# First output product started inside the last attention items; shift, gate and final rows loaded by SP before the experts

## The chip, the cores and the metric

The kernel runs on one core of one Trainium2 chip. The metric is the device time of one execution in microseconds (us). Engines: PE is TensorE (matmuls and transposes), DVE VectorE, ACT ScalarE, POOL GpSimd, SP SyncE. SP computes nothing; it issues DMAs.

## What is computed

Two decoder layers over 640 tokens: 512 latent tokens of a sample and 128 prompt tokens, width 1024. Cut to what matters here (one layer, from the reference):

```
h = _rmsnorm(x, P['norm_mix_g'][l]) * (1 + scm) + sm
a, own = _mixer(h, l, P, pos, ctx)          # differential attention, 4 heads, and latent attention, 4 heads
x = x + gm * a                              # a = mixed @ P['w_o'][l], the output projection
h = _rmsnorm(x, P['norm_ffn_g'][l]) * (1 + scf) + sf
f = _swiglu(h, ...) if l % 2 == 0 else _moe(h, ...)   # layer 1: 8 experts, top 2
x = x + gf * f
```

At the end `y = _rmsnorm(x, final_norm_g)`. The six rows sm, scm, gm, sf, scf, gf (shift, scale and gate) come out of the condition vector, one set for the latent tokens and one for the prompt. All matmul operands are float32, split into a high and a low part, so that each product is three matmuls.

## The kernel before

The program is written out by hand: one block per engine, each a fixed list of instructions with waits on semaphores. The activations of the trunk are kept transposed (features on partitions, tokens along the row). Matmul results go to PSUM, of which three regions of 1024 columns ("main", at 0, 1024 and 2048) are handed out in turn by the table that `plan()` (L212) writes, and a fourth (3072) serves the rest. `claim_main` makes PE wait until the result three places earlier in the table has been read.

**Attention.** Each layer runs two attentions, f = 0 (differential) and f = 1 (latent), of 17 items each (`N_ITEMS`): an item is one head of one tile of 128 queries, and one item takes all four heads of the prompt tile. For an item PE computes scores (L2414), DVE their maximum, ACT the exponentials (L1151, `exp_done`), PE transposes them (L2435, `tr_done`), ACT copies them out (L1197, `pt_ready`), PE multiplies them by the values (L2449, `pv_done`), and ACT copies the result out with its scale (L1173, `pv_evac`). The loop in PE's `attention` (L2459) keeps two items ahead with the scores and issues for item i the values of item i-1 and then the transposes of item i. Of f = 1 all items put the transposes into columns 2048 to 2815 and the values behind them (`turned_at`, `values_at`), so that each waits for the one before to be copied out.

When the items of a query tile are done, `turn_out` (L2553) turns its heads, ACT and DVE split them into `h_hi` and `h_lo` (L1225, L1770, `o_split`). Ten such turns fill the eight k chunks of h: chunks 0 to 3 are the differential heads, which are ready after the first five turns, early in f = 1; chunks 4 to 7 are the latent heads, complete after the last turn (L2583), which follows item 16.

**Output projection.** Then come eight products ("o", l, d), one for each 128 output features (L2601 to L2603). `split_both` (L2284) runs over the 8 chunks of k, three operand pairs and two halves of 320 tokens: 48 matmuls. Before them PE waits for the last turn to be split, and fills that wait: in layer 0 with two throw-away matmuls (`keep_busy`, L2178), in layer 1 with 32 small matmuls that spread the FFN's shift rows over all partitions (L2597); ACT copies these to SBUF (L1245, `shift_row`). After each product DVE adds the gated result to x (L1606), ACT takes squares and scales, and both split the weight of the product after next (L1005, L1456).

**Router and experts.** After the last product of layer 1 come the router, the transposed tokens, to which DVE adds the shift rows (L1959), and the tables of slots. The experts run as 17 slots of 128 tokens; each slot streams 18 pieces of up to 1 MB of weights through nine buffers (SP, L801), which ACT and DVE split (L1334, L2013) for PE (L2708 to L2710). SP issues piece n + 9 when piece n has been split. In the last slot POOL loads `fin_row` (the final norm's weight, L965) and the first gate row (L966), gathers ten blocks of slot results (L971), and loads the second gate row (L975). DVE's `update` (L2113) and `last_norm` (L2122) end the program, one token tile after the other.

## Time and profile before

| | us |
|---|---|
| median of 3 runs | 2054.04 (2053.56 to 2054.39) |
| the profiled execution's own time | 2051.91 |
| its span in the trace | 2050.3 |
| first attention item of layer 0 to the end of the output products of layer 1 | 161 to 1168 |
| router and tables | 1168 to 1200 |
| 17 expert slots | 1200 to 2022 |
| final updates and output | 2022 to 2050 |

PE is busy 97% of the span, DVE 75%, ACT 56%, POOL 12%. The table of the page that divides the span into 40 slices shows PE at nine tenths or more in nearly all of them, and DMA at nine tenths or more in all slices of the experts. A stage is therefore read from its own stretch: in which few places PE stands still, and what it runs there that is not part of the result.

### The profile page before, as it was taken

The page shows a single profiled execution, that of the slowest core. Times are in us where ns is not written, and L with a number is a line of the kernel's source. Part 1 is how long each engine was busy: PE and PEld are TensorE (multiplying, and loading weights), DVE is VectorE, ACT ScalarE, POOL GpSimd, SP SyncE. Part 2 cuts the span into 40 slices and gives each one's busy share as a digit, 9 for nine tenths or more (in the row PEclk, how much of TensorE's full clock was granted, in tenths as well). Part 3 has the DMA queues.
Part 4 walks back from the last instruction along what each step waited for, and adds up shares of the span by engine and source line. Part 5 has one row for each costly group of instructions (what it writes and reads, how often), then busy time and mean ns, then how long its engine had stood idle before and what let it go on. Part 6 is the DMA issues. An engine that isn't in the chain of part 4 may idle for free. (4 is left out here: it accounts for less than half of the span.)

```text
span 2050.3 us, 31301 instructions
## 1 busy us (share of the span) xinstructions
PE 1996.1 (97%) x11814; PEld 1775.3 (87%) x11814; DVE 1528.1 (75%) x1709; ACT 1140.7 (56%) x1389; POOL 239.2 (12%) x258
## 2 busy tenths in 40 slices
PE   8999999999999999999999989999999999999997
PEld 4898679999999999989878978888888888888884
DVE  5547676877767775755852479988899988989997
ACT  5217663322212223623864368777778878788774
POOL 1130100000000000121100037000000000100012
PEclk9999999999999999999999999999999999999999
DMA  9220432344453443321000089999999999999995
GB/s 340 77 90 6 146 113 93 114 164 149 134 169 134 155 132 96 125 69 67 1 1 22 7 325 385 386 386 386 386 386 386 386 386 387 386 387 386 386 387 203
DMA packets 267136, 447.17 MB, mean 218 GB/s; under 512 B 12993, under 2 KB 159393, under 8 KB 266881
## 3 DMA queue, kind: packets, MB, share of 16 engines
q1 hardware_dynamic: 246048, 375.74, 51.7%
q0 software_dynamic: 19120, 67.84, 9.1%
q10 hardware_dynamic: 1872, 2.26, 0.3%
q8 instruction: 67, 1.10, 0.2%
q14 instruction: 29, 0.23, 0.0%
HBM read 430.29 MB, written 16.63 MB: 218 GB/s over the span
## 5 line engine op out<-in xcount | busy, mean ns | idle before, releaser
L2013 DVE TENSOR_TENSOR w_lo<-mraw,w_hi 128x1792 fp32r<-128x1792 f32 (+2 forms) x306 | 643.3, 2113 | 89.0 <-ACT w_hi L1334 86.4
L1334 ACT ACTIVATE w_hi<-mraw 128x1792 fp32r<-128x1792 f32 (+2 forms) x306 | 541.6, 1775 | 174.0 <-PE ps L2710 156.7
L2708 PE MATMUL ps<-w_hi,xs_lo 128*128 128x448 f32 (+1 forms) x816 | 310.0, 380 | 4.8 <-DVE w_lo L2013 3.6
L2710 PE MATMUL ps<-w_hi,xs_hi 128*128 128x448 f32 (+1 forms) x816 | 305.0, 374 | 0.0
L2709 PE MATMUL ps<-w_lo,xs_hi 128*128 128x448 f32 (+1 forms) x816 | 304.7, 373 | 0.0
L1456 DVE TENSOR_TENSOR sub_lo<-zone,sub_hi 128x1024 fp32r<-128x1024 f32 (+2 forms) x112 | 128.3, 1147 | 152.0 <-ACT sub_hi L1005 151.8
L2708 PEld LDWEIGHTS ps<-w_hi,xs_lo 128*128 128x128 f32 x816 | 153.3, 188 | 30.2 <-DVE w_lo L2013 11.2
L2710 PEld LDWEIGHTS ps<-w_hi,xs_hi 128*128 128x128 f32 x816 | 153.2, 188 | 19.2
L2709 PEld LDWEIGHTS ps<-w_lo,xs_hi 128*128 128x128 f32 x816 | 153.4, 188 | 17.8
L2284 PE MATMUL ps<-f_hi,sub_lo 128*128 128x320 f32 x704 | 162.2, 312 | 0.7 <-DVE sub_lo L1456 0.7
L2284 PE MATMUL ps<-f_hi,sub_hi 128*128 128x320 f32 x704 | 161.5, 310 | 0.0
L1005 ACT ACTIVATE sub_hi<-zone 128x1024 fp32r<-128x1024 f32 (+2 forms) x112 | 108.9, 974 | 94.2 <-PE ps L2299 93.7
L2284 PE MATMUL ps<-f_lo,sub_hi 128*128 128x320 f32 x704 | 160.8, 309 | 0.0
L2708 PE MATMUL ps<-w_hi,ea_lo 128*128 128x512 f32 x374 | 151.1, 404 | 2.5 <-DVE w_lo L2013 2.5
L2710 PE MATMUL ps<-w_hi,ea_hi 128*128 128x512 f32 x374 | 146.8, 392 | 0.0
L2709 PE MATMUL ps<-w_lo,ea_hi 128*128 128x512 f32 x374 | 146.3, 391 | 0.0
L1703 DVE TENSOR_REDUCE stat<-ps 128x2 f32<-128x1536 f32 (+2 forms) x68 | 90.5, 1334 | 59.9 <-PE ps L2414 57.3
L2284 PE MATMUL ps<-h_hi,sub_lo 128*128 128x320 f32 x528 | 121.9, 312 | 4.7 <-DVE sub_lo L1456 4.1
L2284 PE MATMUL ps<-h_hi,sub_hi 128*128 128x320 f32 x528 | 121.7, 311 | 0.0
L2284 PE MATMUL ps<-h_lo,sub_hi 128*128 128x320 f32 x528 | 121.6, 311 | 0.0
L2284 PEld LDWEIGHTS ps<-f_hi,sub_lo 128*128 128x128 f32 x704 | 119.3, 189 | 0.9 <-issue 0.9
L2284 PEld LDWEIGHTS ps<-f_lo,sub_hi 128*128 128x128 f32 x704 | 119.7, 189 | 0.0
(368 smaller groups left out, 3667.8 us busy)
## 6 DMA issues: line engine op xcount, KB each, us to landing
mraw<-in_moe_w_down SPq DMA_DIRECT2D x68, 1024.0 KB, 14.5
mraw<-in_moe_w_gate SPq DMA_DIRECT2D x68, 896.0 KB, 13.0
mraw<-in_moe_w_up SPq DMA_DIRECT2D x68, 896.0 KB, 13.1
in_cos<-in_w_mods POOLq DMA_DIRECT2D x72, 512.0 KB, 3.7
mraw<-in_moe_w_gate SPq DMA_DIRECT2D x34, 1024.0 KB
mraw<-in_moe_w_up SPq DMA_DIRECT2D x34, 1024.0 KB
mraw<-in_moe_w_down SPq DMA_DIRECT2D x34, 768.0 KB, 14.7
zone<-in_w_in SPq DMA_DIRECT2D x13, 1024.0 KB, 5.2
```

The source lines that it names most:

```text
L1005: nc.scalar.activation(sub_of(HI, q), raw_w, ACT.Copy).then_inc(t_hi, 1)
L1334: nc.scalar.activation(w_hi[:, n % SPLITS, a], mraw[:, n % MRING, a], ACT.Copy).then_inc(w_hi_ready, 1)
L1456: nc.vector.tensor_tensor(sub_of(LO, q), raw_w, sub_of(HI, q).bitcast(f32), ALU.subtract).then_inc(t_split, 1)
L1703: nc.vector.tensor_reduce(to, sc[..., 0:nk], AXX, ALU.min).then_inc(max_ready, 1)
L2013: nc.vector.tensor_tensor(w_lo[:, n % SPLITS, a], mraw[:, n % MRING, a], w_hi[:, n % SPLITS, a].bitcast(f32), ALU.subtract).then_inc(w_spl ...
L2284: ins = nc.tensor.matmul(ps[:, o + 512 * half:o + 512 * half + wide], a[:, k - k0, :], b[:, k, TH * half:TH * half + wide], start=k == 0 a ...
L2708: nc.tensor.matmul(out, a_lo, b_hi, start=start, stop=False)
L2709: nc.tensor.matmul(out, a_hi, b_lo, start=False, stop=False)
L2710: return nc.tensor.matmul(out, a_hi, b_hi, start=False, stop=stop)
```

## The change

- The first output product ("o", l, 0) no longer runs in one piece. `first_out(k0, k1)` issues the chunks k0 to k1 of it: chunk 0 beside item 14, chunk 1 after the last item, chunks 2 and 3 after the last turn, chunks 4 to 7 when the last turn is split. It owns the main region at 1024 in both layers (`left_out` entries in the table).
- The transposes of item 16 are issued one step earlier, beside item 15, and into columns 0 to 767, its values behind them. They no longer wait for the copies of items 14 and 15. ACT copies them out right after those of item 15 (`turned`).
- The filler of layer 0 and the 32 shift matmuls of layer 1 with ACT's two copies are gone. SP stores the two shift rows to DRAM as four-byte elements, waits for them, and loads each spread over 128 partitions.
- SP loads both gate rows into `in_cos` (free once layer 1's rotary embedding is done) and `fin_row` after the last output product. POOL's three loads and its wait are gone; DVE waits for all of them once, at the first update.

```diff
-        if l:
-            for c in range(2):
-                m(("shift_row", c), "shift_row_ready", c + 1)
+        while len(main_freed) % 3 != 1:
+            left_out()
...
+    shift_rows = nc.dram_tensor("shift_rows", (2, D_MODEL), f32).ap()
...
-        gate_row = [xs, zone[:, xs_at:xs_at + D_MODEL]]
+        gate_row = [in_cos[:, c * D_MODEL:(c + 1) * D_MODEL] for c in range(2)]
...
-        def turned_at(f):
-            return 3072 if f == 0 else 2048
-
-        def values_at(f, lat):
-            return turned_at(f) + 768 if lat else ADA_AT
+        def turned_at(f, i=0):
+            return 3072 if f == 0 else 0 if i == N_ITEMS - 1 else 2048
+
+        def values_at(f, lat, i=0):
+            return turned_at(f, i) + 768 if lat else ADA_AT
...
+            for c in range(2):
+                sp.dma_start(shift_rows[c].rearrange("(k p) -> p k", p=P), mod[:, 1, 24:32, c], allow_slow_non_contiguous=True).then_inc(shift_rows_moved, 16)
+            sp.wait_ge(shift_rows_moved, 32)
+            sp.wait_ge(pv_evac, items_before(DEPTH, 0))
+            for c in range(2):
+                sp.dma_start(shift_row[c], shift_rows[c].partition_broadcast(P)).then_inc(shift_rows_moved, 16)
+            sp.wait_ge(rope_done, 9 * DEPTH)
+            sp.wait_ge(cond_gates, 48)
+            for c in range(2):
+                sp.dma_start(gate_row[c], gate_rows[c].partition_broadcast(P)).then_inc(rows_in, 16)
+            sp.wait_ge(main_done, MAIN[("o", 1, KC - 1)] + 1)
+            sp.dma_start(fin_row, d["fin"]).then_inc(rows_in, 16)
             sp.wait_ge(slots_ready, 1)
-            sp.wait_ge(main_done, MAIN[("o", 1, KC - 1)] + 1)
             e0 = expert(0)
...
             pool.dma_start(yslots[s * P:(s + 1) * P, :], ybuf).then_inc(y_stored, 16)
             pool.wait_ge(y_stored, 16 * (s + 1))
             pool.sem_inc(y_left, 1)
-            pool.wait_ge(cond_gates, 48)
-            pool.wait_ge(etr_done, 2 + G_ETR + 5 * s + TR_OF["xb"] + 1)
             pool.wait_ge(xs_in, 16 * (SLOTS - 1))
-            pool.dma_start(fin_row, d["fin"]).then_inc(rows_in, 16)
-            pool.dma_start(gate_row[0], gate_rows[0].partition_broadcast(P)).then_inc(rows_in, 16)
             pool.wait_ge(row_at_ready, 1)
...
-            pool.wait_ge(pc_done, pieces_done(SLOTS - 1, EPIECE_AT["up", 2, 4]))
-            pool.dma_start(gate_row[1], gate_rows[1].partition_broadcast(P)).then_inc(prompt_gate_in, 16)
-            pool.wait_ge(prompt_gate_in, 16)
...
+                    def turned(i):
+
+                        nt, o = 6 if item(f, i)[2] else len(item(f, i)[1]), turned_at(f, i)
+                        nc.scalar.activation(pt_buf[:, i % 2, 0:nt, :], ps[:, o:o + nt * P].rearrange("p (k n) -> p k n", k=nt),
+                                             ACT.Copy).then_inc(pt_ready, 1)
...
-                        nt = 6 if item(f, i)[2] else len(item(f, i)[1])
+                        if f and i == N_ITEMS - 1:
+                            values_out(i - 1)
+                            continue
                         act.wait_ge(tr_done, it + 1)
                         if i:
                             values_out(i - 1)
-                        o = turned_at(f)
-                        nc.scalar.activation(pt_buf[:, i % 2, 0:nt, :], ps[:, o:o + nt * P].rearrange("p (k n) -> p k n", k=nt),
-                                             ACT.Copy).then_inc(pt_ready, 1)
+                        turned(i)
+                        if f and i == N_ITEMS - 2:
+                            act.wait_ge(tr_done, it + 2)
+                            turned(i + 1)
...
                 q = SUB_AT[("o", l, 0)]
                 turned_hi(1, M_TILES[-1], N_TURN - 1)
-                if l:
-                    for c in range(2):
-                        act.wait_ge(main_done, MAIN[("shift_row", c)] + 1)
...
             def add_shift(t):
                 dve.wait_ge(htok_scaled, t + 1)
-                dve.wait_ge(shift_row_ready, 2)
-                nc.vector.tensor_tensor(htok[:, t, :], htok[:, t, :], shift_rows[t], ALU.add).then_inc(htok_ready, 1)
+                dve.wait_ge(shift_rows_moved, 64)
...
                             pe.wait_ge(exp_done, it + 1)
-                        if i:
+                        last = f and i == N_ITEMS - 1
+                        if i and not last:
                             pe.wait_ge(pt_ready, it)
-                        if i > 1:
...
                         if f and i == 0:
                             pe.wait_ge(vm_ready, 2 * l + 1)
...
                         qt, heads, lat = item(f, i)
                         pe.wait_ge(pt_ready, it + 1)
-                        if i:
+                        if i and not (f and i == N_ITEMS - 1):
                             pe.wait_ge(pv_evac, it)
...
                             if f == 0 and i == D_LAT:
                                 latent_keys(1)
-                        transposes(i)
+                        if not f or i < N_ITEMS - 1:
+                            transposes(i)
                         if i == 0 and f:
                             values_ready()
                         beside(i)
+                        if f and i == N_ITEMS - 2:
...
+                    if i == N_ITEMS - 3:
+                        pe.wait_ge(exp_done, items_before(l, 1) + N_ITEMS - 1)
+                        claim_main(("o", l, 0))
+                        pe.wait_ge(o_split, N_TURN * l + TT)
+                        first_out(0, 1)
+
+                def first_out(k0, k1):
+                    return split_both(("o", l, 0), [p[:, k0:k1, :] for p in split_sub(("o", l, 0))], h_hi, h_lo, k0, k1, KC)
 
                 attention(1, last_value_rows, lambda: pe.wait_ge(vm_early, 2 * l + 2), beside, first)
+                first_out(1, 2)
                 turn_out(1, M_TILES[-1], N_TURN - 1)
-
-
-                pe.wait_ge(exp_done, items_before(l + 1, 0))
-                pe.wait_ge(pv_evac, items_before(l + 1, 0))
-                if l == 0:
-                    keep_busy(("o", l, 0), 2, x_t[:, 0, :])
-                else:
-
-                    pe.wait_ge(mod_rows, 2 * len(MODS))
-                    for c in range(2):
-                        claim_main(("shift_row", c))
-                        o = 1024 * (MAIN[("shift_row", c)] % 3)
-                        for k in range(KC):
-                            ins = nc.tensor.matmul(ps[:, o + k * P:o + (k + 1) * P], mod[:, 1, 24 + k, c:c + 1].to_broadcast([P, P]), ident[:],
-                                                   start=True, stop=True)
-                        ins.then_inc(main_done, 1)
+                first_out(2, 4)
                 pe.wait_ge(o_split, N_TURN * (l + 1))
-                for d_ in range(KC):
+                first_out(4, KC).then_inc(main_done, products(("o", l, 0)))
+                for d_ in range(1, KC):
                     claim_main(("o", l, d_))
                     split_both(("o", l, d_), split_sub(("o", l, d_)), h_hi, h_lo, 0, KC, KC).then_inc(main_done, 1)
```

How it moves the instructions, at the places that matter. PE at the end of layer 1's second attention (L2449 values, L2435 transposes, L2553 the turn, L2597 the shift rows, L2284 the product), from the values of item 14 on:

```order
L2449 MATMUL ps<-zone 128x128 [waits pv_evac,pt_ready]
L2449 MATMUL ps<-zone 128x128 x5
L2435 MATMUL ps<-ident,zone 128x128 [waits pv_evac,pt_ready,exp_done]
L2435 MATMUL ps<-ident,zone 128x128 x5
L2553 MATMUL ps<-ident,zone 128x128 [waits pv_evac,o_split]
L2553 MATMUL ps<-ident,zone 128x128 x3
L2449 MATMUL ps<-zone 128x128 [waits pv_evac,pt_ready]
L2449 MATMUL ps<-zone 128x128 x5
L2435 MATMUL ps<-ident,zone 128x128 [waits pv_evac,pt_ready,exp_done]
L2435 MATMUL ps<-ident,zone 128x128 x5
L2449 MATMUL ps<-zone 128x128 [waits pv_evac,pt_ready]
L2449 MATMUL ps<-zone 128x128 x5
```

and the rows that follow these:

```order
L2553 MATMUL ps<-ident,zone 128x128 [waits pv_evac,o_split]
L2553 MATMUL ps<-ident,zone 128x128 x3
L2597 MATMUL ps<-ident,mod 128x128 [waits mod_rows,vm_ready,pv_evac,exp_done]
L2597 MATMUL ps<-ident,mod 128x128 x7
L2597 MATMUL ps<-ident,mod 128x128 [waits uq_out]
L2597 MATMUL ps<-ident,mod 128x128 x7
L2284 MATMUL ps<-h_hi,sub_lo 128x320 [waits t_split,vm_ready,o_split]
L2284 MATMUL ps<-h_hi,sub_lo 128x320
L2284 MATMUL ps<-h_lo,sub_hi 128x320 x2
```

PE with the change (L2457 values, L2443 transposes, L2564 the turn, L2291 the product), from the values of item 14 on:

```order
L2457 MATMUL ps<-zone 128x128 [waits pv_evac,pt_ready]
L2457 MATMUL ps<-zone 128x128 x5
L2443 MATMUL ps<-ident,zone 128x128 [waits pv_evac,pt_ready,exp_done]
L2443 MATMUL ps<-ident,zone 128x128 x5
L2564 MATMUL ps<-ident,zone 128x128 [waits pv_evac,o_split]
L2564 MATMUL ps<-ident,zone 128x128 x3
L2443 MATMUL ps<-ident,zone 128x128 [waits exp_done]
L2443 MATMUL ps<-ident,zone 128x128 x5
L2457 MATMUL ps<-zone 128x128 [waits pv_evac,pt_ready]
L2457 MATMUL ps<-zone 128x128 x5
L2457 MATMUL ps<-zone 128x128 [waits pt_ready]
L2457 MATMUL ps<-zone 128x128 x5
```

and the rows that follow:

```order
L2291 MATMUL ps<-h_hi,sub_lo 128x320 [waits t_split]
L2291 MATMUL ps<-h_hi,sub_lo 128x320
L2291 MATMUL ps<-h_lo,sub_hi 128x320 x2
L2291 MATMUL ps<-h_hi,sub_hi 128x320 x2
L2564 MATMUL ps<-ident,zone 128x128 [waits pv_evac,o_split]
L2564 MATMUL ps<-ident,zone 128x128 x3
L2291 MATMUL ps<-h_hi,sub_lo 128x320 [waits t_split]
L2291 MATMUL ps<-h_hi,sub_lo 128x320
L2291 MATMUL ps<-h_lo,sub_hi 128x320 x2
L2291 MATMUL ps<-h_hi,sub_hi 128x320 x2
L2291 MATMUL ps<-h_hi,sub_lo 128x320 x2
```

The transposes of item 16 stand ahead of the values of item 15 and wait only for its exponentials; the values of item 16 follow at once; the shift matmuls have gone and chunks of the product stand on both sides of the turn. One more chunk stands ahead of the first of these rows, right behind the transposes of item 14:

```order
L2443 MATMUL ps<-ident,zone 128x128 [waits pv_evac,pt_ready,exp_done]
L2443 MATMUL ps<-ident,zone 128x128 x5
L2291 MATMUL ps<-h_hi,sub_lo 128x320 [waits o_split,t_split,vm_ready,exp_done]
L2291 MATMUL ps<-h_hi,sub_lo 128x320
L2291 MATMUL ps<-h_lo,sub_hi 128x320 x2
L2291 MATMUL ps<-h_hi,sub_hi 128x320 x2
```

SP between the last weights of the output projection and the experts, before (L805 gate rows to DRAM, L801 expert weights):

```order
L769 DMA zone<-in_w_o 128x8x256 [waits t_split] x4
L805 DMA gate_rows<-mod 128x8x1 [waits mod_rows]
L805 DMA gate_rows<-mod 128x8x1
L792 TENSOR_LOAD slot_i [waits main_done,slots_ready]
L792 ISA x2
L801 ISA
L801 DMA mraw<-in_moe_w_gate 128x4x448
```

and SP there with the change (L808 and L812 shift rows, L816 gate rows, L818 the final weight):

```order
L770 DMA zone<-in_w_o 128x8x256 [waits t_split] x4
L806 DMA gate_rows<-mod 128x8x1 [waits mod_rows]
L806 DMA gate_rows<-mod 128x8x1
L808 DMA shift_rows<-mod 128x8x1 x2
L812 DMA zone<-shift_rows 128x1024 [waits pv_evac,shift_rows_moved]
L812 DMA zone<-shift_rows 128x1024
L816 DMA in_cos<-gate_rows 128x1024 [waits cond_gates,rope_done]
L816 DMA in_cos<-gate_rows 128x1024
L818 DMA zone<-in_fin 128x1024 [waits main_done]
L793 TENSOR_LOAD slot_i [waits slots_ready]
```

Seven DMAs and four new waits (`shift_rows_moved`, `pv_evac`, `rope_done`, `cond_gates`) stand between the gate rows' stores and the slots' table, and the wait for the last output product has moved ahead of the final weight.

POOL in the last slot, before (L965 the final weight, L966 a gate row, L971 gathers):

```order
L959 DMA yslots<-zone 128x1024 [waits y_evac]
L965 DMA zone<-in_fin 128x1024 [waits y_stored,xs_in,etr_done,cond_gates]
L966 DMA zone<-gate_rows 128x1024
L971 DMA zone<-yslots,row_at 128x1024 [waits w_split,row_at_ready]
L971 DMA zone<-yslots,row_at 128x1024
L971 DMA zone<-yslots,row_at 128x1024 [waits w_split]
```

and POOL there with the change (L979 gathers):

```order
L971 DMA yslots<-zone 128x1024 [waits y_evac]
L979 DMA zone<-yslots,row_at 128x1024 [waits y_stored,w_split,row_at_ready,xs_in]
L979 DMA zone<-yslots,row_at 128x1024
L979 DMA zone<-yslots,row_at 128x1024 [waits w_split]
L979 DMA zone<-yslots,row_at 128x1024
```

The two loads ahead of the gathers have gone.

## Rows read from the trace of the kernel before

**Rows 1.** The page, its first line.

```profile
span 2050.3 us, 31301 instructions
```

**Rows 2.** PE in order of time, end of layer 0: start, us, instruction, [idle before <-releaser].

```profile
295.78 1.60 PE L2449 MATMUL ps<-zone 128*128 128x128 f32 x12 [1.16 <-ACT zone L1197]
...
299.19 1.60 PE L2449 MATMUL ps<-zone 128*128 128x128 f32 x12 [0.72 <-ACT zone L1197]
...
302.61 1.60 PE L2449 MATMUL ps<-zone 128*128 128x128 f32 x12 [1.16 <-ACT zone L1197]
304.77 0.63 PE L2553 MATMUL ps<-ident,zone 128*128 128x128 f32 x4 [0.55 <-ACT zone L1173]
305.23 1.88 PE L2178 MATMUL ps<-x_t,ones 128*128 128x512 f32 x4
306.81 0.59 PE L2284 MATMUL ps<-h_hi,sub_lo 128*128 128x320 f32 x2
```

**Rows 3.** The same, end of layer 1.

```profile
1100.78 1.60 PE L2449 MATMUL ps<-zone 128*128 128x128 f32 x12 [0.72 <-ACT zone L1197]
...
1106.35 0.63 PE L2553 MATMUL ps<-ident,zone 128*128 128x128 f32 x4 [0.55 <-ACT zone L1173]
1106.81 3.74 PE L2597 MATMUL ps<-ident,mod 128*128 128x128 f32 x32
1110.31 0.55 PE L2284 MATMUL ps<-h_hi,sub_lo 128*128 128x320 f32 x2
```

**Rows 4.** ACT in order of time, end of layer 0.

```profile
296.56 0.90 ACT L1151 ACTIVATE zone<-ps,stat 128x768 f32<-128x768 f32 x1
...
298.34 0.80 ACT L1197 ACTIVATE zone<-ps 128x768 f32<-128x768 f32 x1
```

**Rows 5.** DVE in order of time, end of layer 0.

```profile
293.40 1.22 DVE L1456 TENSOR_TENSOR sub_lo<-zone,sub_hi 128x1024 fp32r<-128x1024 f32 x1
...
306.07 0.69 DVE L1770 TENSOR_TENSOR h_lo<-ps,h_hi 128x512 fp32r<-128x512 f32 x1 [4.51 <-ACT h_hi L1225]
```

**Rows 6.** The chain of waits: start, us, what; layer 1's output products.

```profile
1110.55 57.08 PE ps L2284 x384
```

**Rows 7.** The gate rows' stores (L805), instruction and landing.

```profile
L805 SPq DMA_DIRECT2D gate_rows<-mod x2: 590/928/1266, 1100.0 to 1100.7; - x2
...
DMA to landing us min/median/max: 11.4/12.3/13.2
```

**Rows 8.** SP and DVE in order of time, router.

```profile
1185.55 0.97 SPq L801 DMA_DIRECT2D mraw<-in_moe_w_gate  x2
```

**Rows 9.** DVE in order of time, the first use of a shift row.

```profile
1178.24 1.23 DVE L1959 TENSOR_TENSOR zone<-zone 128x1024 f32<-128x1024 f32 x1
```

**Rows 10.** POOL in order of time, last slot.

```profile
1980.93 0.54 POOL L965 DMA_DIRECT2D zone<-in_fin  x1 [6.83 <-DMA yslots<-zone]
1981.45 0.54 POOL L966 DMA_DIRECT2D zone<-gate_rows  x1
```

**Rows 11.** POOL's gathers of slot results (L971).

```profile
L971 POOL DMA_INDIRECT zone<-yslots,row_at x10: 941/2036/2787, 1993.5 to 2013.6; - x10
```

**Rows 12.** Stretches: busy us of PE, PEld, DVE, ACT, POOL, granted PE clock, DMA share, GB/s.

```profile
1500.00:1547.84 47.84, 47.84 (x230) 41.21 (x230) 43.02 (x28) 38.08 (x29) 3.64 (x3) 1.00 1.05 386
2015.00:2020.00 5.00, 2.54 (x7) 1.82 (x6) 4.64 (x4) 3.40 (x5) 0.14 (x1) 0.75 0.82 317
```

**Rows 13.** ACT in order of time, the last piece of weights.

```profile
2013.34 1.92 ACT L1334 ACTIVATE w_hi<-mraw 128x2048 fp32r<-128x2048 f32 x1 [2.97 <-DMA mraw<-in_moe_w_down]
```

**Rows 14.** PE in order of time, the last piece's matmuls and the final ones.

```profile
2017.79 0.76 PE L2708 MATMUL ps<-w_hi,ea_lo 128*128 128x512 f32 x1 [2.46 <-DVE w_lo L2013]
...
2022.09 1.88 PE L2779 MATMUL ps<-zone,ident 128*128 128x512 f32 x4
```

**Rows 15.** The chain of waits, two of the last piece's twelve matmuls.

```profile
2018.56 0.43 PE ps L2709
...
2021.57 0.23 PE ps L2708
```

More of the change, by code:

```diff
@@ L1160, in values_out @@
                         act.wait_ge(pv_done, it + 1)
[L1161 removed]
+                        o = values_at(f, lat, i)
                         if f == 0:
@@ L1952, in flat @@
                 return a.rearrange("p t e o -> p t (e o)")
-            shift_rows = [shift_row[t // (TT - 1)] for t in range(TT)]
+            shift_of = [shift_row[t // (TT - 1)] for t in range(TT)]
             def add_shift(t):
                 dve.wait_ge(htok_scaled, t + 1)
-                dve.wait_ge(shift_row_ready, 2)
-                nc.vector.tensor_tensor(htok[:, t, :], htok[:, t, :], shift_rows[t], ALU.add).then_inc(htok_ready, 1)
+                dve.wait_ge(shift_rows_moved, 64)
+                nc.vector.tensor_tensor(htok[:, t, :], htok[:, t, :], shift_of[t], ALU.add).then_inc(htok_ready, 1)
             link(nc.vector.tensor_tensor(cmp_a[:], by_o, by_e, ALU.is_gt))
@@ L2426, in transposes @@
                             pe.wait_ge(exp_done, it + 1)
-                        if i:
+                        last = f and i == N_ITEMS - 1
+                        if i and not last:
                             pe.wait_ge(pt_ready, it)
-                        if i > 1:
+                        if i > 1 and not last:
                             pe.wait_ge(pv_evac, it - 1)
@@ L2475, in attention @@
                         beside(i)
+                        if f and i == N_ITEMS - 2:
+                            transposes(i + 1)
                     values(N_ITEMS - 1)
```

16 lines of the change are left out of this document (6 added, 10 removed).

## The prediction

> **What bounds the kernel now.** I read the page first. Its span is 2050.3 us [rows 1], and PE works nearly all of it, so time can only be won where PE stands still, does filler, or runs at the lower clock. Then I went to the stretches that the change touches. A steady slot of the experts is one of PE and DMA together: PE is busy for all 47.84 us of it at clock 1.00, while the DMA engines are full and bring 386 GB/s [rows 12]. PE in order of time shows the end of the attention in layer 0 as a ladder: values of items 14, 15 and 16 start at 295.78, 299.19 and 302.61, each after an idle of 0.72 to 1.16 us that ended with ACT's copy of the transposes; then come an idle of 0.55, the last turn, 1.88 us of filler, and at 306.81 the first output product [rows 2]. Layer 1 has the same ladder, with 3.74 us of shift matmuls in the filler's place and the product at 1110.31 [rows 3]. In the last slot ACT waits 2.97 us for the last piece of weights [rows 13] and PE 2.46 us for ACT and DVE's split of it [rows 14]. A matmul of that piece then starts 0.43 us after the one before, but 0.23 near its end [rows 15]; the mean granted clock of that stretch is 0.75 [rows 12], a mixture of 1.2 and 2.4 GHz. PE had just stood still.
>
> **Spacings.** A row's duration holds the drain of its last matmul. The turn lasts 0.63 but the filler starts 0.46 after it [rows 2], so the drain is about 0.17: six transposes and values of 1.60 us hold PE about 1.45. Eight output products take 57.08 us [rows 6], one 7.135, and one of its eight chunks of k 0.892.
>
> **Part 1, the end of layer 0.** *Before*, from the start of the values of item 15 (299.19) to the end of the first product (306.81 + 7.13 = 313.94) it is 14.75 us.
> *After*, chunk 0 has been computed beside item 14, in the idle of 1.16 ahead of 295.78 [rows 2]. It must wait for the weight's split, which DVE began at 293.40 and ended at 294.62 [rows 5]; 294.65 + 0.89 = 295.54, which just fits. The transposes of item 16 need only its exponentials, done by about 297.5 [rows 4]; they fill part of the 0.72 idle ahead of 299.19. ACT copies item 15's until 299.14 and item 16's by about 299.9 (0.80, [rows 4]), before PE has done the values of item 15 at 300.64. So the values of 16 follow without a gap. The path is: values 1.45 + values 1.45 + chunk 1 0.89 + turn 0.46 + chunks 2 and 3 1.78 + chunks 4 to 7 3.57 = 9.60. Two waits have to be covered. The last turn needs ACT's copy of item 16's values, 0.55 of idle before [rows 2]; chunk 1 lasts 0.89. Chunks 4 to 7 need the split of the last turn, which took from 305.23 to the end of DVE's part at 306.76, 1.53 us [rows 2, 5]; chunks 2 and 3 last 1.78. The gain is 14.75 - 9.60 = **5.15 us**. Both covers are thin, 0.3 us each. If chunk 0 came too early for its weight, or ACT's copies met the split of an earlier turn, 1 to 2 us would be lost: bounds 3 to 5.3.
> All that follows (residual, squares, the next weights' splits) hangs on a product's end and moves with it.
>
> **Part 2, the end of layer 1.** Before: 1100.78 to 1110.31 + 7.13 = 1117.44, 16.66 us [rows 3]. After: the same 9.60. Gain **7.06 us**, of which the missing shift matmuls are 3.5 less the split that they covered; bounds 5 to 7.3.
>
> **Part 3, the last slot.** POOL's two loads, 0.5 MB each (128 x 1024 float32), go out at 1981, into engines that are full [rows 10, 12]; 1.05 MB at 386 GB/s are 2.7 us, which all weights behind them are late. The ten gathers (5 MB) stay [rows 11]. Without the two, ACT's 2.97 falls to 0.3, and PE's idle of 2.46 is nearly gone. PE would start the last piece at 2017.79 - 2.62 = 2015.17, and not having stood still would run its twelve matmuls at 0.23 each: 2.76, end 2017.9 instead of 2022.09 [rows 14, 15]. Gain **4.2 us**, 2.6 of it the wait, 1.6 the clock. Bounds: 0 (the piece is late from the gathers alone, which keep their place) and 4.3. I take the upper value since the lateness and the bytes agree to 0.3 us.
> The Trainium skill ("DMA: Bandwidth & Descriptors", section "Issuing engines are not separate DMA queues") says that DMAs run on the same engines whichever engine issued them, so that moving them to SP alone saves only issue time. By that rule it is the new time that gains here, outside the full stretch, and not the new queue; the trace says nothing against it.
>
> **Part 4, SP.** New between the gate rows' stores (1100 to 1100.7, [rows 7]) and the experts are two stores, five loads and waits; about 0.5 us of issue each by [rows 8, 10], 3.5 in all. The two gate stores, 4-byte elements as well, land after 11.4 to 13.2 us [rows 7]. Four may take that (if latency) up to 26 (if throughput): the shift stores are done at 1114 to 1127. The shift rows are loaded by then to 1140 at the slowest, taking the same 13.2 for a load. DVE first adds one at 1178.24 [rows 9], 1166 with the gain; SP issues the first expert weights at 1185.55 [rows 8], 1173 then. Behind the waiting SP are only these weights, so nothing is late: cost 0, covered by over 25 us. The fin load goes out at the end of the last output product, 1167.6 - 12.2 = 1155 [rows 6], and shares the DMA with nothing large until 1173.
> Against this part speaks a rule of the Trainium skill (same page, section "Rules for kernel authors"): a non-contiguous last dimension becomes one descriptor per element, to be avoided. By it the 1024-element stores are dear, and the rows' 11.4 to 13.2 us for 4 KB agree; it would change the sum only beyond the 25 us of cover.
> ACT's two copies of shift rows and DVE's extra wait at the first update cost nothing: all three loads landed 800 us before.
>
> **Sum.** 5.15 + 7.06 + 4.2 = 16.4 us. The profiled execution took 2051.91 us by its own time, span and 1.6 around it; it would take 2035.5. The median of the runs is 2054.04, 2.1 above that execution; with the same difference **2037.6 us**.
>
> **Rivals.**
> *A, the forecast*, all three gains: 2036 to 2039. Chance 0.62.
> *B, the last slot keeps its wait.* The piece is late because the gathers take DMA time behind POOL, up to 2013.6 [rows 11], and the low clock comes with the wait: only 12.2 gained, 2041.8. For it: ten gathers of 0.5 MB in 20 us are five times the bytes removed. Against: 2.7 us removed beside 2.97 us of wait. 0.17.
> *C, only part of the ends.* Chunk 0 delays the values of item 14 in both layers, or the turn waits behind the shared ACT: 3 to 4 us lost of 12.2, with half of term 3 lost too: about 2045. For it: margins of 0.15 to 0.3 us. Against: all are fixed durations. 0.10.
> *D, the clock.* The filler kept PE active while it waited. If the split still comes late and PE stands there, the first products might run at 1.2 GHz as in the last slot, 0.43 for 0.23 [rows 15]: each us of that costs half of it, some 3.5 for a stretch of a product: 2041. Against: PE has less idle than before, since products fill it. 0.04.
> The Trainium skill ("TensorE: Matmul & The Clock Gate", section "What's actually happening") says that the default state is the throttled one and activity releases it; by that rule removing filler is a risk wherever nothing takes its place.
> *E, it does not do what it says*: the slots or the DMA set the end whatever PE wins before them, or what is gained returns as a wait at 1173 to 1200: within 0.2% of 2054. 0.03.
> *F, slower.* The chained stores and loads hold SP, and with it the expert weights or the shift rows. The mechanism decides once the shift rows land over 16.4 + 4.1 = 20.5 us after 1166, that is after 1186.5, 86 us behind the stores' issue; the four stores strictly one after the other at 13.2 us each, with a load behind them, are 66 us: rows at 1167, a cost of 1 us. At twice that, 132 us, they land at 1233, 67 us late, 51 more than is gained: 2105. Nothing in [rows 7] points there, since two stores landed within 1.8 us of each other. 0.04.
>
> **How the numbers follow.** A measurement of this kernel tells about 0.2% (4.1 us) from no change. A to D are all faster by more: 0.93. Same 0.03, slower 0.04. The predicted time is A's, 2037.6. The range goes from 2035.0 (all upper bounds, 16.9 us, and once more the 2.1 us by which two executions of one kernel differed here) to 2042.8 (all of B and of D, and A with one of its terms at its lower bound); C's slow half, E and F are left out, about 0.15.
>
> **What would show it.** PE in order of time: from the values of item 15 to the end of the first product 9.6 us in both layers, no idle over 0.3 in it, and chunk 0 ahead of item 14's values without delaying them. ACT's wait for the last piece under 0.5 us, PE's spacing there 0.23, clock 1.00. The shift stores landing by 1127, and SP's first expert weights at 1173. Wrong would be: idle ahead of chunks 4 to 7, values of item 14 later than 3.42 after those of 13, a wait of over 2 us for the last piece, or DVE waiting for `shift_rows_moved`.

## The result, and the profile after

The changed kernel takes 2034.29 us in the median of 4 runs (2033.44 to 2035.12), the kernel before 2054.03 beside it: ratio 0.9904, 95% interval 0.9887 to 0.9921. That is 19.7 us less where I had forecast 16.4, and 0.7 us below the range. Over all its executions on record, 79, the kernel before took 2048.9 to 2056.6 us with a mean of 2052.6; ten executions of the changed kernel took 2033.4 to 2035.1 with a mean of 2034.4. The gain is nearer to 18.2 us (side by side in experiment 1 it is 17.6 in the mean), and the four first runs of before lay high. One execution in the experiments, of experiment 8, took 4013.31 us, about twice as long as all others, for a reason that nothing here shows; it is left out.

The granted clock in the rows below is the mean over a stretch: 1.00 is 2.4 GHz throughout, 0.50 is 1.2 GHz throughout, and what lies between is a mixture.

The page after begins with this line, against [rows 1]:

```profile
span 2032.1 us, 31227 instructions
```

PE in order of time, end of layer 0, against [rows 2] (L2457 values, L2443 transposes, L2564 turn, L2291 first product):

```profile
294.72 0.53 PE L2291 MATMUL ps<-h_hi,sub_lo 128*128 128x320 f32 x2
...
295.40 0.45 PE L2291 MATMUL ps<-h_hi,sub_hi 128*128 128x320 f32 x2
295.74 1.60 PE L2457 MATMUL ps<-zone 128*128 128x128 f32 x12
...
298.27 0.82 PE L2443 MATMUL ps<-ident,zone 128*128 128x128 f32 x6
299.16 2.94 PE L2457 MATMUL ps<-zone 128*128 128x128 f32 x24
301.86 0.54 PE L2291 MATMUL ps<-h_hi,sub_lo 128*128 128x320 f32 x2
...
302.84 0.60 PE L2564 MATMUL ps<-ident,zone 128*128 128x128 f32 x4
303.19 0.54 PE L2291 MATMUL ps<-h_hi,sub_lo 128*128 128x320 f32 x2
```

Chunk 0 runs from 294.72 and the values of item 14 start at 295.74 (295.78 before): it cost nothing. The transposes of item 16 stand at 298.27, and the values of items 15 and 16 have become one row of 24 matmuls without idle. From 303.19 on the product runs without a gap. The same at the end of layer 1, against [rows 3]:

```profile
1093.80 2.94 PE L2457 MATMUL ps<-zone 128*128 128x128 f32 x24
1096.50 0.54 PE L2291 MATMUL ps<-h_hi,sub_lo 128*128 128x320 f32 x2
...
1097.47 0.60 PE L2564 MATMUL ps<-ident,zone 128*128 128x128 f32 x4
1097.83 0.53 PE L2291 MATMUL ps<-h_hi,sub_lo 128*128 128x320 f32 x2
```

The last slot, ACT's splits of the two last pieces, against [rows 13]:

```profile
1992.84 1.92 ACT L1343 ACTIVATE w_hi<-mraw 128x2048 fp32r<-128x2048 f32 x1 [0.55 <-PE ps L2716]
...
1996.58 1.92 ACT L1343 ACTIVATE w_hi<-mraw 128x2048 fp32r<-128x2048 f32 x1 [0.30 <-PE ps L2716]
```

ACT no longer waits for a DMA there but for PE, which reads the buffers. PE in order of time at the end of the same piece, against [rows 14]:

```profile
2001.08 0.42 PE L2714 MATMUL ps<-w_hi,ea_lo 128*128 128x512 f32 x1
...
2003.62 0.40 PE L2716 MATMUL ps<-w_hi,ea_hi 128*128 128x512 f32 x1
2003.85 1.88 PE L2785 MATMUL ps<-zone,ident 128*128 128x512 f32 x4
```

It starts at 2001.08 with no idle, its twelve matmuls lie 0.23 apart, and the final matmuls begin 2.77 us later. The stretch 2000:2005 has a granted clock of 1.00.

SP between the attention and the experts, against [rows 7, 8]:

```profile
1095.10 3.02 SPq L808 DMA_DIRECT2D shift_rows<-mod  x2
1112.73 0.81 SPq L812 DMA_DIRECT2D zone<-shift_rows  x2
1113.64 0.85 SPq L816 DMA_DIRECT2D in_cos<-gate_rows  x2
1153.37 0.33 SPq L818 DMA_DIRECT2D zone<-in_fin  x1
1171.25 0.98 SPq L802 DMA_DIRECT2D mraw<-in_moe_w_gate  x2
```

The shift rows' stores land after 15.2 to 15.4 us, a quarter more than the gate rows' of [rows 7]; the loads go out at 1112.7 and land after 4.7 to 6.1. DVE's first addition stands at 1163.95, 45 us later, and the first expert weights at 1171.25, 14.30 earlier than before.

**Where the 18.2 us of span went.** I measured five stretches of PE's row of events in both profiles, each from the start of one named instruction to that of another:

| stretch | before | after | gain |
|---|---|---|---|
| values of item 15, layer 0, to first gate product | 299.19 to 367.69 | 299.16 to 362.23 | 5.43 |
| first gate product to values of item 15, layer 1 | 367.69 to 1100.78 | 362.23 to 1093.80 | 1.52 |
| those values to the last pair of the last output product | 1100.78 to 1167.15 | 1093.80 to 1152.87 | 7.30 |
| to slot 2's first weights (1300.96 and 1287.00) | 133.81 | 134.13 | -0.32 |
| slot 2 to the final matmuls | 1300.96 to 2022.09 | 1287.00 to 2003.85 | 4.28 |

They sum to 18.21. The second row is a surprise: the change touches nothing there. Behind the wait of 1.79 us ahead of the first gate and up products of layer 0, the kernel before ran for some 3.5 us at 1.2 instead of 2.4 GHz (pairs of matmuls 0.53 us apart instead of 0.30); its rows in order of time are:

```profile
367.69 0.54 PE L2284 MATMUL ps<-f_hi,own_lo 128*128 128x320 f32 x2 [1.79 <-DVE own_lo L1456]
...
368.73 0.78 PE L2284 MATMUL ps<-f_hi,own_lo 128*128 128x320 f32 x2
369.31 0.73 PE L2284 MATMUL ps<-f_lo,own_hi 128*128 128x320 f32 x2
```

and its stretches, with the columns of [rows 12]:

```profile
365.00:370.00 5.00, 3.21 (x17) 2.80 (x17) 4.76 (x9) 0.24 (x1) 0.53 (x1) 0.89 0.33 110
370.00:375.00 5.00, 5.00 (x28) 5.00 (x27) 4.27 (x7) 3.63 (x5) 0.00 (x0) 0.77 0.00 0
```

The same row and stretches of the changed kernel:

```profile
362.23 0.54 PE L2291 MATMUL ps<-f_hi,own_lo 128*128 128x320 f32 x2 [1.79 <-DVE own_lo L1465]
```

```profile
360.00:365.00 5.00, 3.21 (x20) 2.79 (x20) 4.76 (x10) 0.71 (x2) 0.53 (x1) 1.00 0.33 110
365.00:370.00 5.00, 5.00 (x33) 4.52 (x32) 4.62 (x7) 3.20 (x6) 0.00 (x0) 1.00 0.00 0
```

The idle is the same in both (3.21 of 5 us busy), the clock is not. Before it fell PE had stood still for 1.79 us and then run for 1.0 us with pairs still 0.29 to 0.38 apart.

### The profile page after: what moved, and what is told of

Read it like the earlier page. It is cut to its first block and busy times, and to the rows that moved or that the text cites. A ratio compares the mean times of both kernels' runs of the same rounds, so it can differ in the third digit from the quotient of the medians.

```text
span 2032.1 us, 31227 instructions
## 1 busy us (share of the span) xinstructions
PE 1987.4 (98%) x11778; PEld 1769.8 (87%) x11778; DVE 1527.8 (75%) x1709; ACT 1139.3 (56%) x1387; POOL 238.7 (12%) x255
## 5 line engine op out<-in xcount | busy, mean ns | idle before, releaser
L2291 PE MATMUL ps<-f_hi,sub_lo 128*128 128x320 f32 x704 | 162.2, 312 | 0.7 <-DVE sub_lo L1465 0.7
L2291 PE MATMUL ps<-f_hi,sub_hi 128*128 128x320 f32 x704 | 161.5, 310 | 0.0
L2291 PE MATMUL ps<-f_lo,sub_hi 128*128 128x320 f32 x704 | 160.8, 309 | 0.0
L2291 PE MATMUL ps<-h_hi,sub_lo 128*128 128x320 f32 x528 | 122.1, 312 | 4.9 <-DVE sub_lo L1465 4.1
L2291 PE MATMUL ps<-h_hi,sub_hi 128*128 128x320 f32 x528 | 121.6, 311 | 0.0
L2291 PE MATMUL ps<-h_lo,sub_hi 128*128 128x320 f32 x528 | 121.5, 311 | 0.0
L2291 PEld LDWEIGHTS ps<-f_hi,sub_lo 128*128 128x128 f32 x704 | 119.3, 189 | 0.9 <-issue 0.9
L2291 PEld LDWEIGHTS ps<-f_lo,sub_hi 128*128 128x128 f32 x704 | 119.7, 189 | 0.0
```

The source lines that it names most:

```text
L2291: ins = nc.tensor.matmul(ps[:, o + 512 * half:o + 512 * half + wide], a[:, k - k0, :], b[:, k, TH * half:TH * half + wide], start=k == 0 a ...
```

## The experiments

Times of the edits are set against 2034.4, the mean of the changed kernel's ten runs, or against 2052.6, where the edit is of the kernel before. Experiments 1 to 3, 5, 6, 9, 10 and 13 to 15 bear on the low clock at the gate product. Their expectations weigh four theories: "chance" (it changes between executions of one program), "kernel" or "place" (it belongs to the program), and "moment" (the time at which PE stands still decides).

**1. The changed kernel again.** No edit.

> The changed kernel once more, nothing edited. Open after the result: the profiled executions differ by 18.2 us of span, of which 1.4 us lies in neither end nor tail: before, PE's matmuls of the first gate and up products of layer 0 start 0.53 us apart per pair (granted clock 0.77 in 370:375) behind an idle of 1.79 us; after, 0.30 behind the same idle. Theory chance: whether that idle costs a stretch at the low clock changes from one execution to the next of the same kernel, so the times lie in two groups about 1.5 us apart (2033.5 and 2035.0), and this profile may show the low clock. Theory kernel: it belongs to the place of the idle in the program; the profile shows clock 1.00 there again and the times do not fall into groups.

Median 2034.62 us (2033.37 to 2035.03), ratio 0.9914 (0.9901 to 0.9928). Clock 1.00 at the gate product once more, but two groups of times (2033.4 and 2033.6; 2034.6 to 2035.0), which theory "kernel" had excluded. Theory "chance" expected two such groups and a low clock in some executions only; the profiled execution is the fastest of the five, so it fits. It does not prove the theory, as one profile can't show that it changes.

**2. Filler in the wait, with the change.** Ahead of `project_group([("gate", 0), ("up", 0)], ...)`:

```diff
+                                keep_busy(("gate", 0), 2, x_t[:, 0, :])
```

> The changed kernel, with two throw-away matmuls of 512 columns (1.6 us, as the removed filler) in PE's 1.79 us wait ahead of layer 0's first gate and up products. Theory chance: the low clock can no longer follow there, the times lie near the lower group, 2033.5, spread under 1 us if this is the main source of spread. Theory kernel: equal to the changed kernel within 0.3 us, 2034.3, since there was no low clock to avoid. If the filler is late for the split it hides behind, up to 0.5 us slower.

Median 2035.32 (2033.83 to 2035.42): no gain, 0.5 us slower in the mean. In its profile the clock stood at 1.00 there, but at 0.50 in 1160:1165, in the router. Filler at one place did not narrow the times.

**3. The same filler in the kernel before.** The line of experiment 2.

> The kernel before with the same filler in the same wait. Both theories let the low clock of 368.7 to 372.4 go: profile 1.00 there. Theory kernel: about 1.5 us faster than before in every run, 2052.5. Theory chance: some 0.7 us faster in the median, and the lowest time that of before.

Median 2050.43 (2047.54 to 2052.52) beside 2052.17 of before; the ratio 0.9993 has the interval 0.9984 to 1.0002, so it is unclear whether it is a gain, though it points to the 1.5. The profile has PE at 1.00 from 365 to 375.

**4. The last slot as before.** SP's loads of the gate rows and the final weight out, POOL's three loads and waits back:

```diff
-            sp.dma_start(fin_row, d["fin"]).then_inc(rows_in, 16)
...
+            pool.dma_start(fin_row, d["fin"]).then_inc(rows_in, 16)
+            pool.dma_start(gate_row[0], gate_rows[0].partition_broadcast(P)).then_inc(rows_in, 16)
```

> The changed kernel with only the last slot as before: POOL loads the final weight and the gate rows, SP's three loads are gone. My term 3: 4.2 us slower than the changed kernel, 2038.5, with ACT waiting some 3 us for the last piece of weights. Rival B (the gathers cause the wait): no slower, 2034.3.

Median 2039.65 (2038.02 to 2041.53), 5.3 us slower. ACT, in order of time, waits for the piece again:

```profile
1999.66 1.91 ACT L1345 ACTIVATE w_hi<-mraw 128x2048 fp32r<-128x2048 f32 x1 [3.34 <-DMA mraw<-in_moe_w_down]
```

and PE:

```profile
2004.12 0.76 PE L2718 MATMUL ps<-w_hi,ea_lo 128*128 128x512 f32 x1 [3.07 <-DVE w_lo L2024]
2004.68 0.63 PE L2719 MATMUL ps<-w_lo,ea_hi 128*128 128x512 f32 x1
...
2008.94 0.63 PE L2720 MATMUL ps<-w_hi,ea_hi 128*128 128x512 f32 x1
2009.37 1.92 PE L2789 MATMUL ps<-zone,ident 128*128 128x512 f32 x3
```

Here all twelve matmuls run at the lower clock, 0.43 apart, 5.25 us for the piece against 4.30 in [rows 14], and the wait is 0.6 longer. Rival B is out: without the two loads the wait is gone although the gathers stay, and these start at nearly the same moment, 1979.16 here and 1979.41 in the changed kernel. The third load of POOL, the second gate row, goes out at 2000.49, after the piece has landed.

**5. The kernel before again.**

> The kernel before once more, nothing edited, for a second profile. By now the times of the kernel before lie between 2049.2 and 2055.1 us, those of the changed kernel between 2033.4 and 2035.1. Theory place (the low clock at 368 to 372 belongs to the kernel before): this profile has PE's first gate and up matmuls of layer 0 at the lower clock again, about 0.77 in 370:375, and the last slot's wait of some 2.5 us followed by a clock under 1.00. Theory chance: the clock at 370:375 is 1.00 here, and the low stretch lies elsewhere.

Median 2053.51 (2048.89 to 2054.67), ratio 1.0002 to itself (0.9993 to 1.0011). Its profile shows the low clock at the gate product again (0.79 in 365:370, 0.87 in 370:375), which favoured theory "place".

**6. Seven throw-away matmuls with the change.** Ahead of the last chunks of the first product:

```diff
+                if l == 0:
+                    keep_busy(("o", l, 1), 7, x_t[:, 0, :])
                 first_out(4, KC).then_inc(main_done, products(("o", l, 0)))
```

> The changed kernel with seven throw-away matmuls of 512 columns (5.5 us) ahead of chunks 4 to 7 of the first output product of layer 0, so that the wait of 1.79 us ahead of the gate and up products lies again where it lay in the kernel before, 365.9 to 367.7. If the moment at which PE stands still decides whether the clock falls, 370:375 shows a low clock as in the kernel before and the time is 5.5 + 1.6, 2041.6 us. If not, 5.5 more than the changed kernel, 2040.0, with 1.00 there.

Median 2039.66 (2039.30 to 2048.22; the slowest of the six had a mean granted clock of 0.947 against 0.995 to 0.997 in the others). The matmuls took 0.86 each, so the idle began at 366.5, 0.6 later than aimed at. Clock 1.00 behind it.

**7. The first product in one piece.** Chunk 0 beside item 14 is out too.

```diff
-                first_out(1, 2)
                 turn_out(1, M_TILES[-1], N_TURN - 1)
-                first_out(2, 4)
                 pe.wait_ge(o_split, N_TURN * (l + 1))
-                first_out(4, KC).then_inc(main_done, products(("o", l, 0)))
+                claim_main(("o", l, 0))
+                first_out(0, KC).then_inc(main_done, products(("o", l, 0)))
```

> The changed kernel without the filling: product (o, l, 0) runs whole behind the last turn's split, no filler in the wait; the early transposes stay. By my steps: values 2.70, idle 0.55 ahead of the turn, turn 0.46, split 1.53, product 7.13 = 12.4 us against 9.5, so 2.9 more in each layer, 5.8 in all: 2040.2. If the clock falls behind PE's wait of some 1.4 us (rival D), up to 3.5 more.

Median 2040.48 (2039.92 to 2041.46), 6.1 slower. PE in order of time:

```profile
299.38 2.94 PE L2457 MATMUL ps<-zone 128*128 128x128 f32 x24
302.87 0.63 PE L2564 MATMUL ps<-ident,zone 128*128 128x128 f32 x4 [0.55 <-ACT zone L1178]
304.92 0.56 PE L2291 MATMUL ps<-h_hi,sub_lo 128*128 128x320 f32 x2 [1.41 <-DVE h_lo L1779]
```

The idle of 0.55 ahead of the turn and of 1.41 ahead of the product are back, and the clock stayed at 1.00 (the pairs behind lie 0.30 apart). The filling is worth what I had worked out, and rival D did not come.

**8. The shift rows late.** SP's stores and loads of the shift rows moved behind the load of the final weight.

```diff
             sp.dma_start(fin_row, d["fin"]).then_inc(rows_in, 16)
+            for c in range(2):
+                sp.dma_start(shift_rows[c].rearrange("(k p) -> p k", p=P), mod[:, 1, 24:32, c], allow_slow_non_contiguous=True).then_inc(shift_rows_moved, 16)
+            sp.wait_ge(shift_rows_moved, 32)
+            for c in range(2):
+                sp.dma_start(shift_row[c], shift_rows[c].partition_broadcast(P)).then_inc(shift_rows_moved, 16)
```

> The changed kernel with SP's shift-row stores and loads behind the last output product (issued at about 1153 instead of 1095). With stores landing after some 15 us and loads after some 5, the shift rows land at about 1177, 14 us after DVE's first shift addition stands at 1164. DVE works in order, so the slots' table and the expert weights are late by as much: my rival F's mechanism, 13 to 14 us slower, 2048. Rival: only SP's hold counts, as SP would issue the first expert weights at 1173 instead of 1171: 2 us slower, 2036.5.

Median 2039.21 of three (2038.78 to 2039.54), some 5 slower: neither forecast. The chain of waits runs where rival F said:

```profile
1154.20 11.85 DMA shift_rows<-mod
...
1166.43 4.69 DMA zone<-shift_rows
1171.26 1.22 DVE zone L1968
...
1184.40 11.02 DMA token_rows<-zone
```

Stores (11.85 to landing), loads (4.69), DVE's addition, the token rows, weights. DVE waits 6.80 us, SP issues the first weights at 1176.79 instead of 1171.25, 5.5 later. The mechanism is shown; its size was wrong. The rows landed at 1171.1 and not at about 1177: with nothing on the queue just ahead of them but the final weight, the stores landed 3.4 us sooner than behind the gate rows' (15.3), and the forecast's own steps (1154.2, 15.3 and 4.7) give 1174 and not 1177. DVE had also stood idle for 1.68 us right behind that addition in the changed kernel. In the changed kernel it has 45 us of cover.

**9. Six throw-away matmuls**, otherwise as 6.

```diff
+                    keep_busy(("o", l, 1), 6, x_t[:, 0, :])
```

> The changed kernel with six throw-away matmuls (5.2 us) at the place where delay5 had seven. So far the low clock behind the wait ahead of the gate and up products stood in both profiles of the kernel before, whose idle began at 365.9 and 365.7, and in none with the change, with the idle at 360.4, 364.0 or, in delay5, 366.5. Theory moment (a sub-microsecond shift of the idle decides): the idle begins here at 365.6, as in the kernel before, so the low clock is back, some 1.5 us, and the time is 2034.6 + 5.2 + 1.5 = 2041.3. Theory kernel (something in the changed kernel keeps the clock up): clock 1.00 there, 2039.8.

Median 2039.33 (2038.69 to 2040.56). The idle lies where it lay in the kernel before, and the stretches are:

```profile
365.00:370.00 5.00, 3.21 (x21) 2.79 (x20) 4.76 (x9) 0.57 (x1) 0.53 (x1) 1.00 0.35 110
370.00:375.00 5.00, 5.00 (x33) 4.52 (x32) 4.69 (x8) 3.30 (x5) 0.00 (x0) 1.00 0.00 0
```

So the moment by the trace's own time does not decide.

**10. Three filler matmuls in the kernel before** instead of two (L2178).

```diff
-                    keep_busy(("o", l, 0), 2, x_t[:, 0, :])
+                    keep_busy(("o", l, 0), 3, x_t[:, 0, :])
```

> The kernel before with three filler matmuls instead of two at the end of the attention of layer 0: 0.8 us more work, which moves the idle to begin at about 366.6, as in delay5. Theory moment: no low clock behind it, so the kernel gets faster by 0.7 us although it does more, 2051.7 in the mean against 2052.4. Theory kernel: the low clock stays, 0.8 slower, 2053.2.

Median 2053.10 (2051.04 to 2054.75), ratio 0.9999 (0.9991 to 1.0008). The low clock was there (0.87 and 0.79), and the added 0.8 us can't be told from nothing beside a spread of 6.4 in the kernel before run with it.

**11. The transposes of item 16 at their old place**, the chunks left in; `turned_at` gives column 2048 for all items of f = 1, and ACT copies item 16 in its own turn.

```diff
-                        if not f or i < N_ITEMS - 1:
-                            transposes(i)
+                        transposes(i)
...
-                        if f and i == N_ITEMS - 2:
-                            transposes(i + 1)
```

> The changed kernel with the transposes of item 16 at their old place and in their old columns; the chunks of the first product stay. The values of item 16 start 3.42 us after those of item 15 again instead of 1.35: 2.1 us more in each layer, 4.1 in all, 2038.7 us. With whole_first (5.9 measured beside 5.8 expected) the two parts would then make 10 of the 12.4 us of the ends.

Median 2037.41 (2035.57 to 2041.31), 3.0 slower. PE in order of time:

```profile
298.99 1.60 PE L2451 MATMUL ps<-zone 128*128 128x128 f32 x12 [0.72 <-ACT zone L1194]
...
302.41 1.60 PE L2451 MATMUL ps<-zone 128*128 128x128 f32 x12 [1.16 <-ACT zone L1194]
303.77 0.54 PE L2285 MATMUL ps<-h_hi,sub_lo 128*128 128x320 f32 x2
```

3.42 us lie between the values again. In its profile the last output product ends 3.99 us later than with the change (its last pair at 1156.86 against 1152.87), the forecast 4.1; 2.0 came back in the router, where this execution had the clock at 1.00 in 1160:1170 and the forty transposes took 4.6 us. The four executions lie 5.7 us apart.

**12. One throw-away matmul in the router** of the changed kernel, in place of the bare claim of ("token_sq",):

```diff
-            claim_main(("token_sq",))
+            keep_busy(("token_sq",), 1, x_t[:, 0, :])
```

> The changed kernel with one throw-away matmul of 512 columns (0.86 us) in PE's wait of 0.36 us for the squares in the router. After the small matmuls there (1157.3 to 1160) the clock stood at 1.2 GHz for 1.7 or 3.4 us of lost time in every profile with the change: the 40 transposes take 6.2 us instead of 4.6. If the extra matmul keeps the clock up, 0.5 us are paid and 1.7 or more won: 2033.3. If not, 0.5 slower, 2035.0.

Median 2035.56 (2032.45 to 2036.87), 0.7 us slower in the mean if anything; one of its four executions is the fastest of all here. The transposes still take 6.23 us. The profile tells something else, though: at the gate product, 800 us ahead of the edit and in a program that is equal to the changed kernel up to there, the clock was low:

```profile
360.00:365.00 5.00, 3.20 (x17) 2.78 (x17) 4.76 (x10) 0.69 (x2) 0.53 (x1) 0.89 0.35 110
365.00:370.00 5.00, 5.00 (x26) 4.76 (x25) 3.81 (x7) 3.18 (x5) 0.00 (x0) 0.77 0.00 0
```

**13. The filler of the kernel before taken away.**

```diff
-                    keep_busy(("o", l, 0), 2, x_t[:, 0, :])
+                    pass
```

> The kernel before with the two filler matmuls at the end of the attention of layer 0 taken away and nothing put in their place: PE waits 1.5 us there for the split of the last turn. Rival D: the first product starts at the lower clock, 0.53 for 0.30 us per pair of matmuls, up to 3.5 us slower than before, 2056. My forecast for this piece: nothing, as the split sets the start, 2052.6. If the filler has to do with the low clock at 368 to 372, that clock is 1.00 in this profile, as in eight of the nine profiles with the change, and the time 1.5 less, 2051.

Median 2052.60 (2049.00 to 2054.88), ratio 1.0002 (0.9993 to 1.0011): nothing, as forecast. The first product starts at 306.98 behind an idle of 1.60 and its pairs lie 0.30 apart, so rival D is out here too. In this profile of an edit of the kernel before, the clock at the gate product was 1.00. The time did not fall by 1.5 for it: from the last output product to slot 2 this execution took some 1.6 us more than the first profile of before, where the router's clock was lower (0.67 in 1170:1175 against 0.94).

**14 and 15. Both kernels once more, one execution each.**

> The kernel before, nothing edited, a third profile. If the low clock behind the wait ahead of the gate and up products belongs to the kernel before, 365:375 is under 1.00 again (so far 3 of 3 with b_shift). If it is chance, as router_fill's profile suggests, where it stood with the change, it is missing here in some of the profiles.

> The changed kernel, nothing edited, a third profile. Kernel: 360:370 at 1.00 again. Chance: low in some of the profiles; 1 of 9 so far with the change.

2053.97 and 2034.96 us. Low in both; the changed kernel's time belongs to the upper group of experiment 1, the two profiles with 1.00 there (2033.68 and 2033.37 us) to the lower. The changed kernel's stretches:

```profile
360.00:365.00 5.00, 3.19 (x16) 2.77 (x15) 4.76 (x10) 0.76 (x2) 0.53 (x1) 0.83 0.33 110
365.00:370.00 5.00, 5.00 (x27) 4.69 (x26) 3.75 (x6) 3.12 (x4) 0.00 (x0) 0.82 0.02 1
```

From its gate product to the values of item 15 of layer 1 this execution took 733.06 us, as the kernel before did (733.09), and not 731.57.

## Why the prediction was wrong, point by point

**Part 1**: 5.15 forecast, 5.43 measured to the gate product. **Part 2**: 7.06 forecast, 7.30 measured. Every wait that I said was covered was covered. Both are some 0.25 too small. About half is the path after, 9.47 and 9.45 us instead of 9.60: 24 value matmuls in a row start the next work after 2.70, not 2.90, the turn holds PE 0.35 instead of 0.46, and the chunks take 0.2 more. The other half is the first product of the kernel before, which took 7.27 and 7.22 us and not the mean of 7.13. Experiments 7 and 11 show two parts of the gain: without the chunks 6.1 are lost (5.8 forecast), without the early transposes 4.0 of PE's time (4.1 forecast). The third, the shift matmuls, was not tested alone; layer 1 won 1.87 more than layer 0, and the rows give 3.50 for the shift matmuls against 1.58 for layer 0's filler, 1.92 more.

**Part 3**: the mechanism was right, the size was not. The wait went with the two loads (experiment 4). The step that failed here is "Gain 4.2 us, 2.6 of it the wait, 1.6 the clock. Bounds: 0 ... and 4.3": the upper bound was no more than one execution's value. From slot 2 to the final matmuls, versions without the loads took 716.8 to 716.9 us in each of ten profiles; five of the seven with them took 721.1 to 721.7, before_fill 722.8 and tail_back 722.6. Their mean less 716.9 is 4.9, the range 4.2 to 5.9, as the wait lasts 2.5 to 3.9 us and the piece behind it 4.1 to 5.3, by how many of its matmuls run at the lower clock. The stretch at the low clock that follows this wait varies: 6 to 8 of the piece's twelve matmuls in six profiles, all twelve in tail_back.

**Part 4**: cost nothing. The stores took 15 us for 4 KB each; experiment 8 shows what it costs where nothing covers it. The Trainium skill ("DMA: Bandwidth & Descriptors", section "Rules for kernel authors") says that a non-contiguous last dimension becomes one descriptor per element, and gives no price for it. The trace agrees: it holds 4176 packets of 4 bytes from 1096.8 to 1106.2, about the 4096 elements of the four stores.

**Sum and median.** Two steps failed. The first put the forecast 2.1 us too high: "The median of the runs is 2054.04, 2.1 above that execution; with the same difference **2037.6 us**". The 2.1 us are no constant between a profiled execution and the others. They are scatter of the kernel before (5.9 us in the comparison of experiment 1 alone); that of the changed kernel's ten executions is 1.7. The sum without them, 2035.5, would have been 1.1 above the ten runs' mean.

The second put the result outside the range: "The range goes from 2035.0 (all upper bounds, 16.9 us, and once more the 2.1 us". That end had already taken the 2.1 us off, so it fell with the 16.9, the bounds 5.3, 7.3 and 4.3. Part 1 passed its bound (5.43), part 3 its own when set against six of the seven profiles with the loads (mean 4.9), and the clock at the gate product, 1.5 between the two profiles, had no term in the sum: all work between the parts was taken to move along unchanged. Mean against mean the gain is 18.2 and the sum 16.4: of the 1.8 between them parts 1 and 2 make 0.5 and part 3 0.7; the remaining 0.6 lie within the clock's scatter at the gate product and in the router, and I can't attribute them. That 2035.5 comes within 1.1 is in part luck: the profiled execution of before lay 0.7 under that kernel's mean, which hid as much of the 1.8.

**The low clock at the gate product** explains 1.5 of the 18.2 us between the two profiles, and it changes between executions of the same program (experiments 1 and 15); what decides it is not known. Of the profiles in which nothing fills that wait it was low in four of five of the kernel before and its edits, and in two of ten of the changed kernel and its edits. Whether these rates differ in truth is open; experiments 6, 9 and 10 excluded only that the moment in the trace's time decides. It also makes two groups of the changed kernel's times plausible, though the router's clock varies by as much (experiment 2).

**Rivals.** A came as to its three gains, though the time lies below its 2036 to 2039. B and D fell by experiments 4, 7 and 13, C by the rows at the top, E by the result, F by the 45 us of cover. What was missing among them is that gains of the clock add to those of the schedule: with the wait gone, its low clock goes too, and with it a stretch that varied by 1.7 us. That the rest of the scatter went for this reason is not shown: edits without the wait still lie 5.7 (experiment 11) and 4.4 us (experiment 12) apart.

## What to carry to other kernels

A stall on TensorE can cost more than its length. Here the low clock followed the stalls of 2.5 to 3.9 us in seven profiles of seven, those of 1.79 us in six of fifteen, and those of 1.41 and 1.60 us at the end of layer 0 in neither. Where a stall is that long, count the work behind it at the lower clock, take its length from more than one execution, and let the bound allow for both. A fixed difference between a profiled execution and a median is scatter until shown otherwise; forecast the profile's own time and widen the range on both sides by the spread of the kernel before instead of adding the difference. A range made of the terms' bounds alone leaves out what the sum has no term for. Small loads belong in a stretch where the DMA engines are free even if nobody needs them for 800 us, and the last item of a ladder can be taken out of it when a free PSUM region is at hand.

## What was not expected of the hardware

The same program with the same idle of 1.79 us gave a granted clock of 1.00 in one execution and about 0.8 in another for the stretch behind it, worth 1.5 us. Stores of 4 KB in four-byte elements landed after 10.8 to 15.4 us when four were issued within 5 us (10.5 to 17.8 over all profiles with the change) and after 11.2 to 11.8 when two were issued without others just ahead (10.7 to 13.2 for the gate rows of the kernel before), so they overlap for the most part; experiment 8 would have been better forecast from that.
